# Moving sums, squares, scores and row loads within the engines' orders, and a row-by-row wait in the output projection, in a hybrid trunk layer on one Trainium2 core

## The reference

```python
xn     = rms_norm(h)
proj   = xn @ w_in                       # short conv b, c, h; q, k, v; z; beta, a; two gates
y_sc   = (b * conv(c * h)) @ w_br_sc
o      = gated_delta_chunked(q, k, v, beta, g, state)   # chunks of 64 positions, 8 heads
y_dn   = (rms_norm(o) * silu(z)) @ w_br_dn
h      = h + (sigmoid(gate_sc) * y_sc + sigmoid(gate_dn) * y_dn) @ w_o
x2     = rms_norm(h)
q      = x2 @ w_q                        # 8 heads, two halves of 128
s      = q . sub_keys                    # 128 keys for each half
...                                      # top 16 of each half, top 16 of the 256 sums, softmax
h      = h + sum_k gelu(x2 . U[idx_k]) * gate_k * V[idx_k]
y      = rms_norm(h)
```

## Time and profile before

| | |
|---|---|
| runs, us | 6165.63, 6171.69, 6186.85 |
| median, us | 6171.69 |
| profiled execution | span 6193.2 us (the profile gives no other time of it) |
| PE busy | 5766.3 us, 93% |
| POOL busy | 1924.6 us, 31% |
| DVE busy | 2153.2 us, 35% |
| ACT busy | 1390.7 us, 22% |

### The profile page before, as it was taken

One profiled execution on the slowest core, in us unless ns is written; L12 is line 12 of the kernel. 1 busy time (PEld: TensorE's weight loads), 2 busy tenths in 40 slices (PEclk: granted clock), 3 DMA queues, 4 the chain that ended last, 5 costly groups with the idle time before them and its releaser, 6 DMA issues.

```text
span 6193.2 us, 104519 instructions
## 1 busy us (share of the span) xinstructions
PE 5766.3 (93%) x42614; PEld 5651.9 (91%) x42614; DVE 2153.2 (35%) x3873; ACT 1390.7 (22%) x1757; POOL 1924.6 (31%) x790
## 2 busy tenths in 40 slices
PE   7889999999888878899999999999999999999998
PEld 6888988999888878898999999999999999999998
DVE  6942322221132018969633222222222222222223
ACT  4431111211221112133322121222222121212222
POOL 2322222222232223221233333333333333333332
PEclk9999988999899999999999999999999999999999
DMA  2231112222333221135533222222222222222222
GB/s 93 83 95 59 59 55 71 65 68 80 93 97 124 84 76 65 62 115 174 170 128 109 87 97 87 87 98 87 94 87 98 87 94 87 97 87 87 98 87 82
DMA packets 229483, 564.94 MB, mean 91 GB/s; under 512 B 53520, under 2 KB 102928, under 8 KB 224016
## 3 DMA queue, kind: packets, MB, share of 16 engines
q1 hardware_dynamic: 229136, 559.46, 27.3%
HBM read 488.65 MB, written 70.74 MB: 90 GB/s over the span
## 4 chain that ended last, share of the span: by engine, by line
PE 52%; issue 35%; DVE 6%; POOL 6%; ACT 1%; DVEq 0%; POOLq 0%; DMA 0%; ACTq 0%; SPq 0%
PE ps L1456 50%; POOL wl L546 6%; PE aux L1715 2%; DVE mm L1380 1%; DVE ob L1367 1%; DVE oa L1365 0%; DVE mg L1401 0%; DVE ti L1292 0%; DVE mrall L1293 0%; ACT yh L863 0%; ACT gl L861 0%; PE aux L1475 0%; DVE ti L1300 0%; DVE tv L1289 0%; DVE sel L1331 0%
## 5 line engine op out<-in xcount | busy, mean ns | idle before, releaser
L546 POOL TENSOR_TENSOR wl<-wr,wh 128x1024 fp32r<-128x1024 f32 x786 | 1924.4, 2449 | 4226.5 <-ACT wh L557 4226.5
L1456 PE MATMUL ps<-xh,wh 128*128 128x288 f32 x7968 | 2427.4, 305 | 100.7 <-DVE xl L940 34.2
L1456 PE MATMUL ps<-xl,wh 128*128 128x288 f32 x7968 | 2389.7, 300 | 24.6 <-issue 24.6
L1456 PE MATMUL ps<-xh,wl 128*128 128x288 f32 x7968 | 2378.4, 298 | 0.0
L557 ACT ACTIVATE wh<-wr 128x1024 fp32r<-128x1024 f32 x786 | 832.9, 1060 | 3870.9 <-PE ps L1456 3853.6
L1456 PEld LDWEIGHTS ps<-xh,wh 128*128 128x128 f32 x7968 | 1529.9, 192 | 123.5 <-issue 69.8
L1456 PEld LDWEIGHTS ps<-xl,wh 128*128 128x128 f32 x7968 | 1531.1, 192 | 29.9 <-issue 27.9
L1456 PEld LDWEIGHTS ps<-xh,wl 128*128 128x128 f32 x7968 | 1534.2, 193 | 0.0
L1456 PE MATMUL ps<-yh,wh 128*128 128x288 f32 x4608 | 1383.8, 300 | 32.2 <-DVE dt L1238 24.2
L1456 PE MATMUL ps<-yl,wh 128*128 128x288 f32 x4608 | 1372.5, 298 | 0.0
L1456 PE MATMUL ps<-yh,wl 128*128 128x288 f32 x4608 | 1367.5, 297 | 0.0
(11 more groups left out here) (222 smaller groups left out, 2623.9 us busy)
## 6 DMA issues: line engine op xcount, KB each, us to landing
wr<-in_w SPq DMA_DIRECT2D x786, 512.0 KB, 3.4
gates_s<-gbuf SPq DMA_DIRECT2D x12, 3072.0 KB, 12.0
gtile<-gates_s SPq DMA_DIRECT2D x32, 1152.0 KB, 5.6
qkv<-qkv_s SPq DMA_DIRECT2D x9, 768.0 KB, 4.7
hid_s<-gl SPq DMA_DIRECT2D x20, 288.0 KB, 11.9
gl<-hid_s SPq DMA_DIRECT2D x20, 288.0 KB, 3.8
mg<-in_x SPq DMA_DIRECT2D x4, 1152.0 KB, 10.9
qkv_s<-lo SPq DMA_DIRECT2D x16, 288.0 KB, 3.1
```

Source lines behind the costliest of these rows:

```text
L546: pool.tensor_tensor(wl[u][:, :, :], wr[u][:, :, :], wh[u][:, :, :].bitcast(F32), ALU.subtract).then_inc(S["lo_done"], 1)
L1456: mm_ = pe.matmul(ps[slot][:, half, 0:HT], a[w][:, t, :], b[:, k, cols], start=first and t == tiles_[0] and x == 0, stop=last and t == til ...
```

## The change

Six places, all behind the chunk stage. The same instructions are issued, but for the loops that are peeled in another way and the 15 waits that `merged_ready` adds.

1. SP asks for the head rows of iteration i+1 after the third of iteration i's four gate stores, not after the fourth.
2. SP asks for `hb` and `sgr` of a branch piece ahead of the weight load that stood before them.
3. ACT, in the output projection, squares a row ahead of the two weight conversions that stood before it.
4. PE, in the head gates, runs the first of four products ahead of the two sums.
5. PE starts the output projection when the first merged row is there and waits for each further row at the block that reads it, no longer for all 16 at the start.
6. PE runs the scores of a head one product later: behind the first of the next head's two products, and for the last head behind the first plain product.

```diff
-        def head_load(i):
+        def head_load(i, first):
             for u in range(2):
-                if not isinstance(i, int):
+                if not first:
                     sp.wait_ge(S["go_scaled"], 2 * i + u - 1)
...
+        def gates_and_heads(i, more=True):
             for m in range(4):
...
+                if m == 2 and more:
+                    head_load(i + 1, False)
...
         def half_again(i):
             for u in range(2):
-                loads(HPD2 + i, 1, u)
                 if not isinstance(i, int):
                     sp.wait_ge(S["merged"], 2 * i + u - 1)
                 sp.dma_start(hb[u][:, :], half_d[2 * i + u, :, :]).then_inc(S[f"hb_in{u}"], 16)
                 sp.dma_start(sgr[u][:, :], sig_d[2 * i + u, :, :]).then_inc(S[f"hb_in{u}"], 16)
+                loads(HPD2 + i, 1, u)
...
         def e(i):                                       # ACT
-            his(HPE + 2 * i, 2)
             if not isinstance(i, int):
                 act.wait_ge(S["evacuated1"], EV_E[1] + i)
                 square(1, 2 * i - 1, 1)
-            his(HPE + 2 * i + 1, 2)
+            his(HPE + 2 * i, 2)
             act.wait_ge(S["evacuated0"], EV_E[0] + i + 1)
             square(1, 2 * i, 0)
+            his(HPE + 2 * i + 1, 2)
...
         def gated(i):                                   # PE
+            product(HPD + 4 * i, 0, 0, EV_D[0] + 2 * i, xh, xl, 2)
             for u in range(2):
...
-            for m in range(4):
+            for m in range(1, 4):
...
-        pe.wait_ge(S["mg_lo"], KD)
+        def merged_ready(k):
+            pe.wait_ge(S["mg_lo"], k + 1)
...
-            product(HPE + 2 * i, 0, 0, EV_E[0] + i, xh, xl, 2)
+            product(HPE + 2 * i, 0, 0, EV_E[0] + i, xh, xl, 2, merged_ready if first else None)
...
+        product(HPF, 0, 0, EV_F[0], xh, xl, 2, chunk_ready(1))
+        product(HPF + 1, 0, 1, EV_F[1], xh, xl, 2)
         pe.wait_ge(S["keys_in"], 16)
-        peel(pe, H, queries)
+        product(HPF + 2, 0, 0, EV_F[0] + 1, xh, xl, 2)
+        scores(0, True)
+        product(HPF + 3, 0, 1, EV_F[1] + 1, xh, xl, 2)
+        with pe.Fori(2, H) as h:
+            product(HPF + 2 * h, 0, 0, EV_F[0] + h, xh, xl, 2)
+            scores(h - 1)
+            product(HPF + 2 * h + 1, 0, 1, EV_F[1] + h, xh, xl, 2)
...
-        for k in range(PLAIN):
+        product(HPG, 0, 0, EV_G[0], xh, xl, 2)
+        scores(H - 1)
+        for k in range(1, PLAIN):
```

More of the change, by code:

```diff
@@ L431, in head_load @@
                 sp.dma_start(gz[u][:, :], z_d[2 * i + u, :, :]).then_inc(S[f"go_in{u}"], 16)
-        def gates_and_heads(i):
+        def gates_and_heads(i, more=True):
             for m in range(4):
@@ L439, in gates_and_heads @@
                 sp.dma_start(sig_d[4 * i + m, :, :], sgd[u][:, :]).then_inc(S[f"sig_kept{u}"], 16)
-        head_load(0)
+                if m == 2 and more:
+                    head_load(i + 1, False)
+        head_load(0, True)
         gates_and_heads(0)
-        with sp.Fori(1, H // 2) as i:
-            head_load(i)
+        with sp.Fori(1, H // 2 - 1) as i:
             gates_and_heads(i)
+        gates_and_heads(H // 2 - 1, False)
         for u in range(2):
@@ L1672, in _, with scores @@
         norm_sum(1, KD - 1, 1, stop=True)
[L1674 to L1677, removed]
+        def scores(h, first=False):
             for u in range(2):
                 pe.wait_ge(S[f"evacuated{u}"], EV_F[u] + h + 1)
-            if not isinstance(h, int):
+            if not first:
                 pe.wait_ge(S["scores_read"], h)
```

## The result

Four runs of the changed kernel gave 5983.38, 5999.75, 6001.38 and 6003.09 us, a median of 6000.57; four of the kernel before a median of 6173.15. The ratio is 0.9708, with a 95% interval of 0.9689 to 0.9727: 172.6 us faster. The profiled run of the changed kernel is the one of 5999.75 us; its span is 195.2 us shorter than that of the profile before, which was the execution of 6193.2 us.

A forecast was written before the change was run, and what follows sets the result against it. TensorE, busy 93% of 6193.2 us, was taken as the bound, with time to gain only from its pauses and low clock. Savings of 55.8 + 35.3 + 11.9 + 37.0 + 3.4 = 143.4 from 6171.69 gave 6028.3 us, range 6008 to 6064.

The forecast's parts named there:

- The change touches none of the last.: Expert loop, last of TensorE's eight stretches, 97% busy at clock 0.99: the change was forecast to save 0 us there.
- No matmul, copy or byte is added; things stand elsewhere: Whole change: claimed to only rearrange existing work; no time of its own was given.
- Head gates: Gates stage: product ahead of the sums and earlier row loads end the waits for squares, 55.8 us less.
- the sum: All stages together: 143.4 us less than before.
- rival 3: Head gates: rows still late, only the first iteration's 11.2 of 55.8 us remain, 6073 us; chance 0.04.
- Branch product and the gap: Second half of the branch product: earlier rows, 35.3 us less, 3 us allowed; gap behind it: 11.9 less.
- Output projection: Output projection: squares ahead of weight conversions end 14 waits of 1.78 us and low clock, 37.0 us less.
- Rival 1: Output projection: ScalarE's queue becomes the bound, each product waits again, 24.9 us back, 6053 us; chance 0.07.
- Scores: Queries and scores: scores one product later, one plain product fewer behind them, 3.4 us less.
- 2: Branch and output products: the clock doesn't recover though the pauses go, 14.1 + 9 us back, 6051; chance 0.06.
- 4: Branch product: bound by weights queued behind row loads instead, 35.3 us lost, 6064 us; chance 0.05.
- 5: Expert loop: almost unbroken work lowers its clock from 0.99 to 0.94, costing 183 us, 6212; chance 0.02.

## Why the prediction was wrong, point by point

**The step that failed** is the sentence on the expert loop in the first part: "The change touches none of the last." None of its instructions was touched, but the loop was moved, and the twelve jumps back cost 7.5 us each at its old place and 3.6 at its new one. 47.4 us of the profiles' 195.2 are this, 38 to 40 in the medians of the runs that moved the loop alone. The signs were in the trace of before: 24 waits for issue, 58.7 us, all behind 3500 us. I had listed the waits only up to 2700 us and read the loop from one line of windows, busy 97% at 0.99; the 92 us without work in that line I asked nothing about. And "No matmul, copy or byte is added; things stand elsewhere" was true of the work, not of the program, which became 425 instructions longer ahead of the loop.

**Head gates**: right, 54.1 for 55.8, 53.1 us an iteration for 53.2, first wait for weights 2.23 us. That the two edits cover mostly the same wait I had not worked out; it would not have changed the sum. But it makes rival 3's price wrong: with the rows asked for late 45 of the 54 us stayed, where it left 11.2 of 55.8.

**Branch product and the gap**: right, 37.9 for 35.3 and 11.9 for 11.9. The 3 us allowed for the first rows were not needed. The gap's cause was shared: 5.8 us of it go to the row by row wait, the rest to the rows asked for earlier.

**Output projection**: right, 37.7 for 37.0; a period of 13.75 us, of which the sum is 0.95 for the 1.0 that I took. Rival 1, the queue of ScalarE with a margin of 0.7 to 1.7 us, did not come about: no wait for `wl` in the stage. The split was less complete: beside the waits and the low clock (6.4 us by four long periods before, 3.2 by two with the third edit taken back) there is the slower start behind each wait, 14 times 0.26 us, which I had no term for.

**Scores**: right, 4.1 for 3.4, with five waits for top-k and one plain product ahead of the last scores.

**The rivals**: 2 fell, the clock stood at 1.00 in both stages. Taking the second edit back brought 0.88 with the waits, so that the low clock did go with the pauses: 1.2 GHz stands behind each of its seven waits of 3.2 to 4.3 us. The Trainium skill (TensorE: Matmul & The Clock Gate, HAM oscillation — how this bites in real kernels) describes a kernel in which the wait between two stretches of matmuls lets the clock fall each time, and these seven agree with it. Behind the waits of 1.78 us it fell more rarely, four times of 14 in the kernel before and two of 14 with the third edit taken back. 3 and 4 fell, since no head rows came late and no branch piece waited for weights. Of 5 the opposite came: the clock of the loop rose from 0.98 to 0.99 as pauses left it, and to 1.00 without any.

**The basis.** The execution profiled before was longer than every run of that kernel shown: of the 195.2 us between the profiles, 22.6 are not in the medians' 172.6. The seven stretches account for all of the 195.2. In the medians the sum and the loop's 38 to 40 would make 181 to 183, 9 to 11 more than was measured; whether that is the spread of the `z` stage (below) no run shows.

## What to carry to other kernels

Ask of a large hardware loop what each jump back costs, by the waits put down to issue and the count of instruction packets in the loop's window: twelve jumps cost 43 to 90 us here, and writing the loop out gave 35 to 43 more than the whole change had. An edit that only adds or removes instructions ahead of such a loop can move the time by 0.6%, so that a comparison of two orders should first hold the place of the loop fixed, or write it out. Take that place from the trace: a count from the source was 20 instructions off here, and that was enough to miss the place. And list the waits over the whole span, also where the change does nothing.

## What the runs showed of the hardware that was not expected

- The second pause comes and goes with the place alone: with 3 to 6 matmuls of the loop in the first packet there are two pauses (2.81 and 2.15 us in the jump shown); in the changed kernel, where 38 to 43 had run before the third packet began to arrive, there is one. At every jump of the two kernels the second packet began to arrive 0.35 to 1.03 us behind TensorE's restart; that it is asked for no earlier is inferred from this. A place at which a jump of this loop costs nothing was not found; no others than those above were tried.
- Not every loop is fetched again. The head gates' loop, some 800 instructions, jumps back twice between 1705 and 1824 us of the changed kernel; no packet of queue 8 arrives there, and TensorE waits for nothing. In the expert loop of 3146, 14 or 15 arrive in each iteration. On instruction fetch the Trainium skill (Runtime: NRT & Kernel Launch, Instruction fetch mechanics) says that blocks of 16 KiB are fetched in order ahead of use, and that a branch to a block not held stalls the engine: the packets and pauses agree. The room of 2048 instructions that it gives TensorE agrees with both loops, since the one that is fetched again is longer and the other shorter. Its remark that only two blocks are held does not, since 800 instructions are more than three.
- Executions of the unchanged part differ. The last `z` product ended between 1581 and 1608 us in the fourteen profiles, at a mean granted clock of 0.94 in the shorter and 0.92 in the longer. That is a spread as wide as that of the runs of one kernel (up to 27 us), and the reason why single totals above say less than the stages.
